# Expert weights of a routed FFN: three weight buffers in place of two, and two blocks of rows on one load for four experts at fixed places of the order

## The reference, cut to what matters

```python
def moe_ffn(xt, rg_w, rg_b, re_w, re_b, w13, w2):
    # 4 groups, then 2 of the group's 8 experts for each token: 1024 rows for 32 experts
    ...
    def expert_block(args):
        xblk, e = args
        gate, up = jnp.split(xblk @ w13[e], 2, axis=-1)
        return (jax.nn.silu(gate) * up) @ w2[e]
    yb = lax.map(expert_block, (xb, blk_exp)).reshape(R, D)
    return jax.ops.segment_sum(yb * row_w[:, None].astype(yb.dtype), row_tok, num_segments=T)
```

## Time and profile before

| what | value |
|---|---|
| median of 3 executions | 2629.65 us (2629.41 to 2632.89) |
| the profiled execution's own time | 2633.32 us |
| its span, first to last instruction | 2631.6 us |
| PE busy, share of the span | 2124.2 us, 81% |
| DVE, ACT, POOL busy | 797.7, 272.3, 274.2 us |
| moved by the queue of SP | 579.96 MB |
| mean granted TensorE clock | 0.906 |

### The profile page before, as it was taken

The page is one execution under the profiler, slowest core; times in us unless marked ns, Lnnn a source line. Parts: engine busy times, 40 slices in busy tenths (PEclk is TensorE's granted clock), DMA queues, the critical chain, the costliest instruction groups (busy, mean ns, idle before and its releaser), DMA issues. The chain is left out here.

```text
span 2631.6 us, 20975 instructions
## 1 busy us (share of the span) xinstructions
PE 2124.2 (81%) x7470; PEld 944.2 (36%) x7470; DVE 797.7 (30%) x1341; ACT 272.3 (10%) x497; POOL 274.2 (10%) x515
## 2 busy tenths in 40 slices
PE   5998999999789487777878479799995777778782
PEld 3553444444334432222222144344454322222220
DVE  3775204534511611111111224255735111111113
ACT  2111212211100100000000031211101000000000
POOL 0000000000000421112111100000003211211110
PEclk8998999999889599999999758899996899999996
DMA  8897322120020689999999420111016699999993
GB/s 322 325 359 265 122 88 96 57 88 8 0 96 0 254 331 421 421 421 420 417 420 411 183 70 0 61 62 66 16 64 251 247 421 421 421 421 419 415 411 118
DMA packets 186146, 618.93 MB, mean 235 GB/s; under 512 B 21928, under 2 KB 39584, under 8 KB 178729
## 3 DMA queue, kind: packets, MB, share of 16 engines
q1 hardware_dynamic: 161310, 579.96, 55.4%
q10 hardware_dynamic: 13260, 21.40, 2.3%
q0 software_dynamic: 11520, 16.83, 1.7%
HBM read 601.76 MB, written 37.33 MB: 243 GB/s over the span
## 5 line engine op out<-in xcount | busy, mean ns | idle before, releaser
L550 PE MATMUL bank<-w,xT0e 128*64 128x512 f32 x1152 | 278.8, 640 | 71.8 <-DMA w<-in_moe_w 71.2
L550 PE MATMUL bank<-w,xT1e 128*64 128x512 f32 x1088 | 261.9, 637 | 71.1 <-DMA w<-in_moe_w 70.5
L550 PEld LDWEIGHTS bank<-w,xT0e 128*64 128x64 f32 x1152 | 93.0, 147 | 256.2 <-issue 206.3
L550 PEld LDWEIGHTS bank<-w,xT1e 128*64 128x64 f32 x1088 | 87.5, 147 | 244.5 <-issue 196.2
L1081 PE MATMUL bank<-uhi,wnh 128*128 128x512 f32 x384 | 168.4, 593 | 0.9 <-ACT uhi L888 0.9
L564 PE MATMUL bank<-w,hT0e 128*64 128x512 f32 x576 | 131.5, 597 | 22.7 <-issue 22.1
L564 PE MATMUL bank<-w,hT1e 128*64 128x512 f32 x544 | 124.2, 597 | 21.5 <-issue 20.9
L1430 PE MATMUL bank<-uT,wo 128*128 128x512 f32 x256 | 132.0, 597 | 0.5 <-DVE uT L1318 0.5
L631 DVE TENSOR_TENSOR hb0e<-sg0e,bank 128x256 f32<-128x256 f32 x36 | 15.2, 421 | 338.4 <-ACT sg0e L607 338.4
L631 DVE TENSOR_TENSOR hb1e<-sg1e,bank 128x256 f32<-128x256 f32 x34 | 14.3, 421 | 321.5 <-ACT sg1e L607 321.5
L1767 PE MATMUL bank<-uT,wo 128*128 128x512 f32 x256 | 111.1, 595 | 0.0
(11 more groups left out here) (525 smaller groups left out, 2517.9 us busy)
## 6 DMA issues: line engine op xcount, KB each, us to landing
w<-in_moe_w SPq DMA_DIRECT2D x70, 4096.0 KB, 23.6
w<-in_moe_w SPq DMA_DIRECT2D x70, 2048.0 KB
adab<-in_ada_w SPq DMA_DIRECT2D x24, 2048.0 KB, 11.3
wnh<-in_h_in_w SPq DMA_DIRECT2D x12, 1024.0 KB, 4.9
wo<-in_m_in_w SPq DMA_DIRECT2D x4, 2048.0 KB, 11.6
wo<-in_m_in_w ACTq DMA_DIRECT2D x4, 2048.0 KB, 20.6
yg<-d_y SPq DMA_DIRECT2D x8, 1024.0 KB, 7.9
d_xm<-xmb ACTq DMA_DIRECT2D x16, 385.5 KB, 6.6
```

The lines of the kernel that those rows point to most:

```text
L550: ins = t_.matmul(b_gu[n * C:(n + 1) * C, :].rearrange("c (g f) -> c g f", g=2), xT[:, k, half * C:(half + 1) * C], w[:, kk, n], start=(kk ...
```

## The change

There are three buffers for w13 and w2 (NB = 3), and `route` loads the weights of experts 0 to 2. `ORDER` is a fixed list of 36 steps over 32 places: the places 3, 10, 17 and 24 have two steps each on one load, with six single places between them. At run time `route` picks the four experts with most rows among experts 3 to 31 and puts them at those places; they have room for 128 rows. Experts 0 to 2 keep the places 0 to 2. Rows beyond an expert's room still go to overflow steps, each with a load. SP reads the expert of each place from `meta`.

All steps are written out one after another for each engine. In `experts`, PE now runs for step s: product 1 of s, the hidden transposes of s - 1, the row transposes of s + 1, product 2 of s - 1; there are three PSUM banks for product 1, and one buffer `yb` for the result in place of two. Behind the 36 steps comes a drain of the last step, and then the overflow steps under conditions. The router's tables have one buffer for both layers, and layer 1's are loaded at the start of the `experts` stage of layer 0. In `route`, `hT` has 2 slices in place of 8, and `junk` and `n2b` lie in `vt`.

```diff
-NBLK = NE + NOV + 2
+NB = 3
+PAIRS = 4
+SOLO = 6
+ORDER = [p for p in range(NE) for _ in range(2 if p >= NB and (p - NB) % (SOLO + 1) == 0 and p < NB + PAIRS * (SOLO + 1) else 1)]
+NS = len(ORDER)
+ORDER += range(NE, NE + NOV)
+LAST = {p: s for s, p in enumerate(ORDER)}
+NBLK = NS + NOV + NB
...
-                    for u in range(2):
-                        sp.dma_start(w13[u][:], w13v[:, u]).then_inc(s_w13[u], 16)
-                        sp.dma_start(w2[u][:], w2v[:, u]).then_inc(s_w2[u], 16)
+                    for u in range(NB):
+                        sp.dma_start(w13[:, u], w13v[:, u]).then_inc(s_w13[u], 16)
+                        sp.dma_start(w2[:, u], w2v[:, u]).then_inc(s_w2[u], 16)
...
-                    if l == 0:
-                        load_route_tables(sp, 1)
...
+                    own(v.scalar_tensor_tensor(out=key[:, NB:], in0=cnt[:, NB:], scalar=float(NE), in1=rev[:, NB:], op0=ALU.mult, op1=ALU.add))
+                    own(v.max(m8[:], key[:]))
+                    own(v.tensor_scalar(isd[:], key[:], m8[:, PAIRS - 1:PAIRS], None, ALU.is_ge))
...
+                    def place(dst_, each):
+
+                        own(v.scalar_tensor_tensor(out=dst_, in0=grp[:], scalar=float(each), in1=idx[:], op0=ALU.mult, op1=ALU.add))
+                        own(v.tensor_scalar(alt[:], rk[:], float(SOLO + each), float(NB), ALU.mult, ALU.add))
+                        own(v.tensor_tensor(alt[:], alt[:], dst_, ALU.subtract))
+                        own(v.tensor_tensor(alt[:], alt[:], isd[:], ALU.mult))
+                        own(v.tensor_tensor(dst_, dst_, alt[:], ALU.add))
...
+                def steps(eng, main, drain, extra):
+
+                    for s in range(NS):
+                        main(s)
+                    drain()
+                    more = eng.value_load(meta[0:1, 0:1], min_val=0, max_val=NOV)
+                    for q in range(0, NOV, 4):
+                        with eng.If(more > q):
+                            for o in range(q, q + 4):
+                                with eng.If(more > o):
+                                    extra(NS + o)
...
+                    def load(p, col):
+
+                        e = sp.value_load(meta[0:1, col:col + 1], min_val=0, max_val=NE - 1)
+                        u, _n = turn(p)
+                        sp.wait_ge(S["up"], LAST[p - NB] + 1)
+                        sp.dma_start(w13[:, u], w13v[:, bass.ds(e, 1)].rearrange("p o k n -> p (o k) n")).then_inc(s_w13[u], 16)
+                        sp.wait_ge(S["yp"], LAST[p - NB] + 1)
+                        sp.dma_start(w2[:, u], w2v[:, bass.ds(e, 1)].rearrange("p o k n -> p (o k) n")).then_inc(s_w2[u], 16)
+
+                    def main(s):
+                        p = ORDER[s]
+                        if p >= NB and s == LAST[p]:
+                            load(p, 1 + p)
...
+                    if l == 0:
+                        load_route_tables(sp, 1)
+                    steps(sp, main, lambda: None, extra)
...
+                    def first(s):
+                        u, n = turn(ORDER[s])
+                        pe.wait_ge(S["xTa"], s + 1)
+                        pe.wait_ge(S["xTv"], s + 1)
+                        pe.wait_ge(s_w13[u], n)
+                        at_least(pe, S["h"], s - NB + 1)
+                        product1(u, b_gu[s % NB])
...
+                    def main(s):
+                        first(s)
+                        if s > 0:
+                            h_transposes(s)
+                        next_rows(s)
+                        if s > 0:
+                            product2(s)
+
+                    def drain():
+                        h_transposes(NS)
+                        product2(NS)
```

More of the change, by code:

```diff
@@ L329, in _ @@
                     ins.then_inc(S["tps"], 1)
+                    pe.wait_ge(S["ecs"], 1)
+                    for i in range(2):
+                        ins = t_.matmul(bank[1][0:1, i * P:(i + 1) * P], ec[:, i:i + 1], ident[:], start=True, stop=True)
+                    ins.then_inc(S["esp"], 1)
                 @blk.vector
@@ new lines, in _ @@
+                    for j in range(1, PAIRS):
+                        own(v.scalar_tensor_tensor(out=grp[:], in0=idx[:], scalar=float(NB + SOLO * j), in1=grp[:], op0=ALU.is_ge, op1=ALU.add))
+                        if j < PAIRS - 1:
+                            own(v.scalar_tensor_tensor(out=rk[:], in0=key[:], scalar=m8[:, j:j + 1], in1=rk[:], op0=ALU.is_lt, op1=ALU.add))
+                    def place(dst_, each):
[4 more added lines that the diff above has]
+                        own(v.tensor_tensor(dst_, dst_, alt[:], ALU.add))
@@ L449, in experts @@
                 blk = c.enter_context(nc.Block())
[L450 to L456, removed]
-                                body(o + MAIN, u)
+                def steps(eng, main, drain, extra):
[8 more added lines that the diff above has]
+                                    extra(NS + o)
@@ new lines, in ahead @@
+                    def ahead(s):
+                        u, n = turn(s)
+                        pool.wait_ge(s_xg[u], n)
+                        pool.wait_ge(S["xps"], s + 1)
+                        gather(u, tokc[:, s + NB:s + NB + 1], s + NB + 1)
+                    def main(s):
+                        ahead(s)
+                        if s > 0:
+                            scatter(s)
+                    def drain():
+                        scatter(NS)
+                        pool.wait_ge(S["yst"], NS * 16)
+                        for s in range(NS, NS + NB):
+                            u, n = turn(s)
+                            pool.wait_ge(s_xg[u], n)
@@ L513, in _, with extra @@
+                    def extra(s):
+                        ahead(s)
+                        scatter(s + 1)
+                        u, n = turn(s + NB)
+                        pool.wait_ge(s_xg[u], n)
+                        pool.wait_ge(S["yst"], (s + 1) * 16)
+                    for u in range(NB):
                         g.memset(xg[u][:], 0.0).then_inc(S["xz"], 1)
-                    pool.wait_ge(S["xz"], 2)
-                    for u in range(2):
+                    pool.wait_ge(S["xz"], NB)
@@ L527, in body @@
-                    def body(it, u):
-                        block(it, u)
-                        pool.wait_ge(s_xg[u], 16 * it + 32)
-                        pool.wait_ge(s_yst[u], 16 * it + 16)
-                    extra(pool, total, body)
+                    steps(pool, main, drain, extra)
                 @blk.tensor
@@ L585, in _, with extra @@
+                    def extra(s):
+                        first(s)
+                        next_rows(s)
+                        h_transposes(s + 1)
+                        product2(s + 1)
                     pe.wait_ge(s_xg[0], 16)
                     x_transposes(0)
-                    for u in range(2):
-                        block(0, u)
-                    with pe.Fori(1, MAIN) as it:
-                        for u in range(2):
-                            block(it, u)
-                    total = pe.value_load(meta[0:1, 0:1], min_val=0, max_val=NOV)
@@ L593, in _ @@
-                    extra(pe, total, block)
+                    steps(pe, main, drain, extra)
                 @blk.scalar
@@ L640, in _, with drain, extra @@
+                    def drain():
+                        h_turned(NS)
+                        y_out(NS)
+                    def extra(b):
+                        hidden(b)
+                        h_turned(b + 1)
+                        y_out(b + 1)
                     x_half(1)
                     dve.wait_ge(s_g2, 32)
-                    for u in range(2):
-                        block(0, u)
-                    with dve.Fori(1, MAIN) as it:
-                        for u in range(2):
-                            block(it, u)
@@ L647, in _ @@
-                    total = dve.value_load(meta[0:1, 0:1], min_val=0, max_val=NOV)
-                    extra(dve, total, block)
+                    steps(dve, main, drain, extra)
         def spectrum(t_, dft, src, dst, g):
```

258 lines of the change are left out of this document (124 added, 134 removed).

## The result

The changed kernel takes 2570.4 us (median of 4, 2569.33 to 2573.89) against 2630.24: ratio 0.9769, 95% interval 0.9756 to 0.9781. It is 60 us faster, where the forecast was 80; the sign and the range (2530 to 2580) held. The profiled execution has a span of 2572.2 us against 2631.6, 59.4 less.

A forecast was written before the change was run, and what follows sets the result against it. Weight loads were taken to bound the experts stages. Terms of -52.0, -38.4, 2 x 4.0, 2 x 0.5 and 1 sum to -80.4 us against 2633.3: 2552.9, less 3.7 for the median, 2549 us; range 2530 to 2580.

The forecast's parts named there:

- the prediction's 4 and 3 loads: Experts stages: 4 fewer loads inside layer 0's stage and 3 fewer in layer 1's, worth 59.8 and 44.8 us.
- an expert's 6 MB at 421 GB/s take 14.94 us: Experts stages: time of one expert's weight load, used as the worth of each load saved.
- a load rate below 421 GB/s: Weight loads: listed among the signs that would prove the prediction wrong.
- PE keeps up: Experts stages: PE takes 11.6 us a step and catches up 3 or 4 places behind a pair, without loss.
- the sign I gave: PE waits for weights at two or three places ahead of each pair, at none of the three behind.
- The rival in which PE becomes the bound: Experts stages: a 13.5 us step makes results 9.5 us later in each layer, 2568 us in all; chance 0.15.
- the start: Start of each experts stage: w2 released late, load queue dry for 2.7 us near +21, in each layer.
- Layer 0's end: Last result of layer 0's experts stage, after the overflow step, at +504.3 against +556.3: 52.0 us less.
- Layer 1's end: Last result of layer 1's experts stage, after the drain, at +488.9 against +527.3: 38.4 us less.
- Route: Route stage: DVE's longer chain costs 4.0 us per layer; the third load, covered by it, costs nothing.
- Stage ends: From last scatter to first load of combine: same time as before, bounds 4 less and 5 more per layer.
- The dear skips of the rival: Stage ends: four jumps over unrun overflow code take 5 us more in each layer, 2559 us; chance 0.12.

The follow-up runs named there:

- E5: E1 without the pairs: 32 steps, one per expert, overflow steps with loads as before; 2609.9 us, ratio 0.9919.
- E1: The changed kernel with 32 bytes of unused room ahead of the weight buffers, so they start at a multiple of 256; 2546.5 us, ratio 0.9671.
- E7: E1 with hidden transposes and product 2 back in their own step, on all engines, and no drain; 2538.3 us, ratio 0.9650.
- E8: E1 with SP issuing loads in the order their buffers come free, w13 ahead of the previous place's w2 except at pairs; 2534.1 us, ratio 0.9635.
- E11: E8 with the four groups of overflow steps nested, so one skip passes all that is left; 2531.5 us, ratio 0.9615.

## Why the prediction was right or wrong

**Right: the loads bound the stage and five of them go.** 65 issues of w13, 548.5 MB. E5 prices the five loads of the pairs at 63 us by the medians and at 68 by the results, 44.1 + 24.3, where five times 14.94 is 74.7. The other two of the prediction's 4 and 3 loads are those that the third buffer moves into route. Three of layer 0's four overflow blocks were taken in, and expert 1's stayed.

**The step that failed: "an expert's 6 MB at 421 GB/s take 14.94 us", carried over to the changed kernel.** The rate was read from the trace before and taken for a property of the load; it was also one of the buffers' address. At 407 GB/s a load takes 15.45, and 30 and 29 loads make 15 us in each layer. E1 gives back 13.5 and 14.3 of them and comes to 2546.5 against the forecast 2549. The diff shows the cause in a part that I gave a cost of 1 us (the router's tables); I priced the moving of the loads and not that of the memory. The prediction named "a load rate below 421 GB/s" as a thing that would prove it wrong, but had no rival for it, so the range held by the width given to others, and that was luck.

**Right: PE keeps up.** 11.52 us for a step against 11.6. No wait stands directly behind a pair (the second step of the pair at 1083.66 and the two starts after it are free; the third, at 1119.70, waits 1.27). That is one place sooner than the sign I gave, none at the three behind. From there on every place up to the next pair waits, four or five and not two or three. The rival in which PE becomes the bound fell: a step stayed under 13.5 us, and E7's is longer by 1 us and the kernel faster.

**Right in place, small in effect: the start.** The gap is in the window where it was put, +21 to +26, with the engines at 0.62 for 5 us: 2 us against 2.7. E8 removes it.

**Layer 0's end.** At the rate of before the result came at +499.8 against +504.3. The last place's product 1 starts at +469.8 in E1, just as forecast, but takes 7.1 us and not the 8.6 I gave it. The 2.5 us for the count and two conditions were nothing on PE's path: product 2 of the drain and product 1 of the overflow step are back to back (1425.66 and 3.65 against 1429.11, above), so the count had been read and the branches taken before the matmuls ahead were through.

**Layer 1's end.** +489.3 in E1 against +488.9 (the terms as given add up to +488.7). Two errors offset each other: the last product 1 starts at +468.9, 1.0 earlier than forecast, and from there to the result it takes 20.4 us in place of 19.0. Of that, 1.3 are the wait of the last result for the scatter ahead of it, which has come with the single `yb` and stood in no term.

**Route.** +4.9 twice against +5.5 and +4.5. DVE's 31 instructions took 7.6 us (902.53 to 910.16 in the changed kernel) against 7.25, as the scans and those with a scalar from memory take 0.23 to 0.25 and not 0.19. The third load was covered, more closely than I had it: in layer 0 the engines are full to 915 and at 0.13 from 915 to 920, and route's last DVE instruction ends at 920.9.

**Stage ends.** Taken as even, they came out 2.1 and 0.2 better. The dear skips of the rival (+5 in each layer) didn't come: E11 puts a skip at 0.3 to 0.5 us. The rule in the Trainium skill ("Runtime: NRT & Kernel Launch", "Instruction fetch mechanics") isn't contradicted by that, but a stall at a skip was at most a part of these 0.3 to 0.5 us here.

**Not decided.** E7 and E8 were not put together, so whether their gains add is open. Nor was the third load's cover in route taken away, which has some 5 us of room.

## What to carry to other kernels

Where a stage is bound by DMA, its price is the bytes, and each load saved comes back nearly in full as long as the queue never runs dry (68 of 75 us here); ask then which buffer is released last and in which order the queue is fed. Work that shortens the engine that waits (here the late product 2, with the loads in the order of E1) is worth nothing and costs a drain. And when a change moves an allocation, check the start address of every large DMA target: a tile removed far from the loads cost them 3%.

## What the runs showed of the hardware

In these runs the rate of large loads from HBM into SBUF depends on the start address within the partition: 4 KB rows at a multiple of 256 bytes run at 420 to 421 GB/s, and at 64, 128 or 224 past one at 407 to 408, all three alike. The DMA engines' busy share reads 1.03 in both. The Trainium skill has a rule that is near it, in "DMA: Bandwidth & Descriptors", section "How a descriptor splits into AXI transactions": each transaction of a transfer has to start at a 256-byte boundary, so that a transfer that starts off one begins at the boundary below and fetches bytes that it doesn't use. By its count of beats (32 bytes each), and with a row of 4096 bytes as one descriptor, I estimate 128 beats for an aligned row and 130, 132 or 135 at the three offsets, losses of 1.5, 3 and 5%. The loss measured is about 3% at each of them, so the count of beats doesn't give it; nor does the count of transactions, 17 in place of 16, which would be 6%. The section speaks of what a transaction reads, and the sources of these loads didn't move; the targets in SBUF did. Why the loss is what it is stays open.

The other surprise is how little the branches of an unrolled kernel cost: 0.3 to 0.5 us at the end of a stage for a skip over four steps' code on all engines, and nothing on PE's path between two runs of matmuls.
